# First MLP of a two-layer decoder trunk: the relu's transpose moved from TensorE to VectorE and ScalarE

## What is computed

```python
def squared_relu_mlp(h, w_up, w_down):
    return jnp.square(jax.nn.relu(h @ w_up)) @ w_down      # 2048 -> 8192 -> 2048

for i in range(DEPTH):                                     # DEPTH = 2
    mod = (silu(c) @ w_ada[i] + b_ada[i])                  # 6 vectors of 2048
    sh_a, sc_a, g_a, sh_m, sc_m, g_m = split(mod, 6)
    h = x * (1 + sc_a) + sh_a
    y = mixer_i(h)                                         # differential / sliding-window attention
    x = layer_norm(ALPHA * x + (1 + g_a) * y)
    h = x * (1 + sc_m) + sh_m
    y = squared_relu_mlp(h, w_up[i], w_down[i])
    x = layer_norm(ALPHA * x + (1 + g_m) * y)
```

## Time and profile before

| | |
|---|---|
| median of 3 runs | 2228.99 us (2226.84 to 2229.18) |
| the profiled execution | 2228.67 us |
| its span | 2226.9 us |
| TensorE busy (PE) | 2168.5 us, 97% |
| VectorE busy (DVE) | 1790.6 us, 80% |
| ScalarE busy (ACT) | 981.3 us, 44% |
| HBM read | 592.60 MB |

### The profile page before, as it was taken

The page is one execution under the profiler, slowest core; times in us unless marked ns, Lnnn a source line. Parts: engine busy times, 40 slices in busy tenths (PEclk is TensorE's granted clock), DMA queues, the critical chain, the costliest instruction groups (busy, mean ns, idle before and its releaser), DMA issues.

```text
span 2226.9 us, 26022 instructions
## 1 busy us (share of the span) xinstructions
PE 2168.5 (97%) x9952; PEld 1791.8 (80%) x9952; DVE 1790.6 (80%) x2057; ACT 981.3 (44%) x1330; POOL 33.4 (2%) x53
## 2 busy tenths in 40 slices
PE   6999999999999999999999999999999999999997
PEld 6887888877888888888888788777888888888886
DVE  6899998887997897888786888777966865874877
ACT  1135444546433443443353655536534443443441
POOL 0001000000000000000000000000000000000000
PEclk9899999999999999999999999999999999999999
DMA  9999888877999999999985643365766676666663
GB/s 360 384 331 347 322 320 300 306 245 256 361 364 325 354 366 335 325 380 350 323 311 190 198 152 119 122 207 190 236 221 223 213 241 206 219 217 219 228 234 113
DMA packets 262592, 596.41 MB, mean 268 GB/s; under 512 B 13426, under 2 KB 14788, under 8 KB 262468
## 3 DMA queue, kind: packets, MB, share of 16 engines
q1 hardware_dynamic: 254800, 579.45, 74.2%
q10 hardware_dynamic: 7668, 15.30, 2.2%
HBM read 592.60 MB, written 2.10 MB: 267 GB/s over the span
## 4 chain that ended last, share of the span: by engine, by line
PE 88%; DVE 7%; DMA 1%; issue 1%; ACT 1%; SPq 0%; DVEq 0%; POOL 0%; ACTq 0%; POOLq 0%
PE pair L1709 25%; PE pair L1711 25%; PE pair L1710 25%; DVE acc L916 2%; DVE w_lo L901 1%; PE pair L1967 1%; PE pair L1969 1%; PE pair L1968 1%; PE pair L1729 1%; PE pair L1731 1%; PE pair L1730 1%; PE turn L2041 1%; DMA y<-in_w_ada_dram 1%; PE turn L2022 1%; PE turn L1603 1%
## 5 line engine op out<-in xcount | busy, mean ns | idle before, releaser
L528 ACT ACTIVATE w_hi<-raw 128x1024 fp32r<-128x1024 f32 x712 | 726.8, 1056 | 620.2 <-PE pair L1711 297.4
L901 DVE TENSOR_TENSOR w_lo<-raw,w_hi 128x1024 fp32r<-128x1024 f32 x712 | 852.5, 1220 | 117.0 <-ACT w_hi L528 110.8
L1709 PE MATMUL pair<-w_hi,h_hi 128*128 128x512 f32 x1456 | 581.3, 399 | 1.5 <-DVE w_lo L901 0.8
L1711 PE MATMUL pair<-w_hi,h_lo 128*128 128x512 f32 x1456 | 567.8, 390 | 0.0
L1710 PE MATMUL pair<-w_lo,h_hi 128*128 128x512 f32 x1456 | 567.3, 390 | 0.0
L1709 PE MATMUL pair<-w_hi,f_hi 128*128 128x512 f32 x1056 | 414.0, 392 | 0.1
L1711 PE MATMUL pair<-w_hi,f_lo 128*128 128x512 f32 x1056 | 411.1, 389 | 0.0
L1710 PE MATMUL pair<-w_lo,f_hi 128*128 128x512 f32 x1056 | 410.9, 389 | 0.0
L929 DVE SCALAR_TENSOR_TENSOR acc<-ada_w,cvec,acc 128x1024 f32<-128x1024 f32 x300 | 383.6, 1279 | 1.8 <-DVE x L1312 0.9
L1709 PEld LDWEIGHTS pair<-w_hi,h_hi 128*128 128x128 f32 x1456 | 273.5, 188 | 62.9 <-DVE w_lo L901 6.3
L1711 PEld LDWEIGHTS pair<-w_hi,h_lo 128*128 128x128 f32 x1456 | 273.2, 188 | 58.4
(11 more groups left out here) (190 smaller groups left out, 1669.5 us busy)
## 6 DMA issues: line engine op xcount, KB each, us to landing
ada_w<-in_w_ada_dram SPq DMA_DIRECT2D x320, 512.0 KB, 6.1
raw<-in_w_up_dram SPq DMA_DIRECT2D x128, 1024.0 KB, 6.1
raw<-in_w_down_dram SPq DMA_DIRECT2D x128, 1024.0 KB, 5.2
raw<-in_a_w_qkv_dram SPq DMA_DIRECT2D x48, 1024.0 KB, 7.6
ada_f<-in_w_ada_dram SPq DMA_DIRECT2D x44, 512.0 KB, 11.5
raw<-in_b_w_qkv_dram SPq DMA_DIRECT2D x20, 1024.0 KB, 5.2
raw<-in_a_w_o_dram SPq DMA_DIRECT2D x16, 1024.0 KB, 6.5
raw<-in_b_w_o_dram SPq DMA_DIRECT2D x16, 1024.0 KB, 5.1
```

Source lines behind the costliest of these rows:

```text
L528: act.activation(w_hi[:, (b.n * SUB + n) % SPLITS], raw[:, slot, k:k + 2], ACT.Copy).then_inc(hi_ready, 1)
L901: dve.tensor_tensor(w_lo[:, slot, k:k + 2], raw[:, slot, k:k + 2], w_hi[:, (b.n * SUB + n) % SPLITS].bitcast(F32), ALU.subtract).then_inc( ...
L1709: pe.matmul(o, hi[:, kt, at], w[:, k], start=kt == 0, stop=False)
L1711: mm = pe.matmul(o, lo[:, kt, at], w[:, k], start=False, stop=kt == KT - 1)
```

## The change

In layer 0 the relu is now transposed without TensorE, in a third way. ScalarE writes the relu to `R` as before. VectorE turns all of it with one instruction, 128x1024, from `R` into the PSUM tensor `turn[:, 0]` (`up_turn`, behind its `split_lo(2)`); every 32x32 square is turned in place. ScalarE then copies sixteen quarter-rows of 32x256 from there to `RR`, which brings the squares to their partitions: eight behind `split_hi(3)`, eight behind `split_hi(4)` (`up_move`), and squares from `RR` behind `split_hi(5)` (before: behind `split_hi(4)`). VectorE's difference stands behind `split_lo(5)` (before: `split_lo(4)`), the relu behind ScalarE's `split_hi(2)` (before: 1). TensorE's `turn_up` is gone.

The modulation pieces of the first MLP follow a table over 31 steps: 4 in each of the first four, 7 or 8 in the four steps with results of down blocks, 6 in the steps with results of up blocks of the later rounds, 4 in the last three. The sums are complete at the steps 4, 7, 9, 11, 14, 16, 18, 21, 23, 25, 28 and after the end (before: 3, 5, 7, 10, 12, 14, 17, 19, 21, 24, 26, 28); only the first ten need an insert on TensorE within the MLP. The table of the second MLP gives the same pieces and sums as the rule did.

```diff
-ON_CHIP = (1,)
+ON_CHIP = (0, 1)
+BY_SCALAR = (0,)
@@
-MLP_BLOCKS = 28
-MLP_ADA = {1: [5], 2: [1, 5], 4: [1, 3, 5, 7], 5: [0, 1, 3, 5, 7], 6: [0, 1, 3, 5, 6, 7], 7: [0, 1, 3, 4, 5, 6, 7]}
+MLP_ADA = {0: [], 1: [5], 2: [1, 5], 4: [1, 3, 5, 7], 5: [0, 1, 3, 5, 7], 6: [0, 1, 3, 5, 6, 7],
+           7: [0, 1, 3, 4, 5, 6, 7], 8: [0, 1, 2, 3, 4, 5, 6, 7]}
+MLP_PIECES = (4 * [4] + [7, 8, 7, 8] + 2 * (4 * [6] + [7, 8, 8, 8]) + 4 * [6] + 3 * [4],
+              [(i + 1) * 32 // 28 - i * 32 // 28 for i in range(28)] + 3 * [0])
@@
-def mlp_pieces(i, halves):
-
-    return (MLP_ADA[(i + 1) * 16 * halves // MLP_BLOCKS - i * 16 * halves // MLP_BLOCKS] if i < MLP_BLOCKS else [])
-
-
-def mlp_sum(i, halves):
-
-    return {-(-MLP_BLOCKS * (k + 1) // halves): k for k in range(halves)}.get(i)
+def mlp_pieces(layer, b):
+
+    return MLP_ADA[MLP_PIECES[layer][b]]
+
+
+def mlp_sum(layer, b):
+
+    before, after = sum(MLP_PIECES[layer][:b - 1]) // KT, sum(MLP_PIECES[layer][:b]) // KT
+    return before if b > 0 and after > before else None
@@ ScalarE
+            def up_move(first, last):
+
+                def run():
+                    act.wait_ge(up_blocks, st.turned.n + 1)
+                    for i in range(first, last):
+                        a, c = i // 4, i % 4
+                        ins = act.activation(by_token(rows32(up_rows(RR), c), a),
+                                             by_feature(rows32(turn[:, 0], a), c), ACT.Copy)
+                    if last == 16:
+                        ins.then_inc(up_moved, 1)
+                return run
@@ ScalarE, mlp
                     if layer in ON_CHIP:
+                        if i < 4 and layer in BY_SCALAR:
+                            hk[3], hk[4] = up_move(0, 8), up_move(8, 16)
                         if i < 4:
                             hk[5] = up_square_there(i)
@@ VectorE
+            def up_turn(b, pp):
+
+                dve.wait_ge(evacuated, b + 3)
+                dve.transpose(turn[:, 0], up_rows(R)).then_inc(up_blocks, 1)
@@ VectorE, mlp
                     if layer in ON_CHIP and i < 4:
-                        hooks[3] = up_turn_rest
-                        block_(before=up_turn_across, later=(5, up_rest(i)), ada=mlp_pieces(b, halves), hooks=hooks)
+                        if layer not in BY_SCALAR:
+                            hooks[3] = up_turn_rest
+                        block_(before=up_turn if layer in BY_SCALAR else up_turn_across, later=(5, up_rest(i)), ada=mlp_pieces(layer, b), hooks=hooks)
```

More of the change, by code:

```diff
@@ L498, in mlp @@
                     src = up(it, i + 1) if i < 3 else down(it, i - 3) if i < 7 else up(it + 1, 0)
-                    load_block(src, mlp_pieces(b, 2 * len(parts)), of)
+                    load_block(src, mlp_pieces(layer, b), of)
             mlp(0)
@@ L802, in mlp @@
                     for half in range(2):
-                        if mlp_sum(b + 2, halves) == gate_at + half:
+                        if mlp_sum(layer, b + 2) == gate_at + half:
                             hk[0] = load_gate_bias(layer, 5, half)
@@ L1462, in mlp @@
                     last = it == QUARTERS - 1
-                    k = mlp_sum(b, halves)
+                    k = mlp_sum(layer, b)
                     hooks = {}
@@ L1472, in mlp @@
                     if layer in ON_CHIP and i < 4:
-                        hooks[3] = up_turn_rest
-                        block_(before=up_turn_across, later=(5, up_rest(i)), ada=mlp_pieces(b, halves), hooks=hooks)
+                        if layer not in BY_SCALAR:
+                            hooks[3] = up_turn_rest
+                        block_(before=up_turn if layer in BY_SCALAR else up_turn_across, later=(5, up_rest(i)), ada=mlp_pieces(layer, b), hooks=hooks)
                         continue
                     block_(before=(down_last if last else down_add)(i - 4) if i >= 4 else None,
-                           later=(4, up_lo(i)) if i < 4 else None, ada=mlp_pieces(b, halves), hooks=hooks)
+                           later=(4, up_lo(i)) if i < 4 else None, ada=mlp_pieces(layer, b), hooks=hooks)
             mlp(0, 1, 0)
```

## The result

| | before | after |
|---|---|---|
| median | 2229.06 us | 2252.41 us (2250.76 to 2253.29) |
| profiled execution | 2228.67 us | 2252.58 us |
| its span | 2226.9 us | 2250.8 us |
| TensorE busy | 2168.5 us | 2166.4 us, 96% |
| VectorE busy | 1790.6 us | 1810.4 us, 80% |

The kernel is slower by 23.4 us: ratio 1.011, 95% interval 1.0098 to 1.0122. The forecast was 2252.5.

What follows compares the result with a forecast made beforehand. TensorE, never dry, was taken as the bound. Removed inserts save 14.4 us, but a VectorE-ScalarE loop longer than the block makes it 38.2 us late: 2228.7 + 23.8 = 2252.5 us, range 2238 to 2268.

Steps and rivals of the forecast that it cites:

- What bounds the kernel, and what goes away: TensorE never runs dry; removing its 16 relu-turn inserts of 0.90 us in the first MLP saves 14.4 us.
- The transpose: VectorE's new 128x1024 transpose from SBUF into PSUM after each up block: 1.25 us, between 1.14 and 1.79.
- The dearer rival: VectorE's transpose into PSUM takes 1.79 us, adding 8.6 us for 2261 us; chance 0.08.
- The copies: ScalarE's sixteen 32x256 copies per up block, held by changing start partitions: 0.40 us apart, bounds 0.27 and 0.42.
- ScalarE's side: First part of the transpose-to-transpose loop: transpose, hand-over, sixteen copies, two splits and squares, 11.76 us.
- the blocks' lateness: TensorE's delay in first-MLP blocks because the loop of 24.6 us exceeds the 21.76 us block: 38.2 us together.
- runs 2, 3 and 4: Groups of four first-MLP blocks after up blocks, with modulation sums; predicted late by 9.2, 9.6 and 8.3 us.
- VectorE's side: Rest of the loop, f_lo and everything queued before the next transpose: 12.8 us, 13.1 in the first four blocks.
- The idle time ahead of L1709: TensorE's waits at a subtile's first matmul line, some 30 to 40 us, all for VectorE's w_lo.
- The DMA: Loads for down blocks with eight pieces: 0, bounds 0 and +8 us; rival that it fails, 2260 us, chance 0.05.
- the residual: VectorE's residual work in the first MLP's last down blocks: 0.7 us more lateness after run 4.
- overlapping copies: Rival: ScalarE's copies start 0.28 us apart, runs late by only 7 us, 2221 us; break-even about 0.307; chance 0.07.

Runs made afterwards that it cites:

- the kernel with both edits: Against the kernel after: up-block modulation pieces moved into VectorE's waits, and the last three steps' pieces 6, 6, 0 instead of 4, 4, 4; 2214.37 us (0.9935).
- the kernel with the same rows: Against the kernel after: four copies in a row keep input and output partitions, so most copy wrong squares; 2229.4 us (1.0005).

## Why the prediction was right, and where it was not

- **What bounds the kernel, and what goes away:** right. 14.4 us for the sixteen inserts: the kernel with both edits has the pieces and the chain hidden and is 14.3 below before.
- **The transpose,** taken at 1.25: sixteen rows of 1.249 to 1.260. The dearer rival is out.
- **The copies,** taken at 0.40 apart: 0.388 on the mean (925.42 - 922.34 = 3.08 and 929.63 - 926.51 = 3.12 for eight). The step was right in kind, held by the start partition, and read off two neighbours of ScalarE with 64 partitions; its size was 0.012 too large. ScalarE's side is 11.57 instead of 11.76: 0.19 in sixteen loops, 3.0 of the 3.7 by which the blocks' lateness was overrated. Another part I had not looked for: a sum begins with the cheaper L943, 0.5 less, which falls into the loop once in each of runs 2, 3 and 4, 1.6 together. In run 4 some of it goes again, since its first transpose starts 1.57 after its block instead of the 1.26 that I took; about 0.6 us of difference is left that is not assigned.
- **VectorE's side,** 12.8 by counting its queue: 12.26 with the cheaper piece, 12.80 without. Waits of 2 to 3 us in the fifth and sixth subtile: 1.92 and 2.98.
- **The idle time ahead of L1709 (now L1732),** foretold as 30 to 40 us: 24.8 for w_lo by the page, 32.0 by starts. The mechanism is there; the rows leave out 0.27 of each wait, as shown above.
- **The DMA,** taken at 0 with up to 8: nothing. The down blocks with 7 and 8 pieces are 21.76 without an insert, in the kernel after as in the one with the table alone.
- **The missing term.** The prediction moved pieces into the last three steps and counted nothing there, except 0.7 for the residual. In the last block, by half steps, w_lo has no lead and VectorE's queue passes two more jobs (L1166, L1168) between them: a piece ahead of a w_lo that TensorE waits for is paid there, and behind the longer wait the clock is lower. Every kernel here with pieces on the last step has both the wait of 3.3 us and the lower clock, and none of the others has either; which of the new wait and the longer one the clock needs was not separated. Together +4.1, and the expectation that single waits stay at 2 us or less and the granted clock at 1 was wrong there. An error of -3.7 and one of +4.1 cancelled: the total of 2252.5 against 2252.41 is closer than the working deserved.
- **The rivals:** overlapping copies would have given 2221 by my sum; the kernel that has them took 2229.4, or 2225.3 without the missing term. Their size was off too: I had eight of them as 8 x 0.28 = 2.24, and the rows of the kernel with the same rows have 2.38 and 2.41 from the first copy to the instruction behind the eight (930.44 to 932.82, 933.90 to 936.31), since the fifth copy is still held by the fourth and what starts behind the eight by the last. That is 0.31 a loop, at most 5 us in sixteen, about the 4 that are missing. Per copy it is a mean of 0.299, at which this change is worth nothing (ratio 1.0005); my sum, which had no missing term, put that point at 0.307.

## What to carry to other kernels

When a job goes off the busiest engine onto two others as a chain (A, then B, then A again), compare the block with the loop, and not with the busy shares: both helpers had room (83% and 55%), and the block was 24.7 instead of 21.76. The remedy is not less work but its place: filler that has no due time belongs behind the instruction at which its engine is going to wait, here a second table of places, 35 us. And look where such filler has no lead to eat, a block by half steps at the end of a stage.

## What was new about the chip

- ScalarE overlaps two copies of 32x256 (0.36 to 0.37 long, 0.27 to 0.28 apart) only if they start in the same partition on input and on output. If either changes, or both, they are 0.37 to 0.39 apart, no less than the 0.37 to 0.38 that one takes.
- VectorE's transpose of 128x1024 from SBUF into PSUM takes 1.255 us and lets the next pass start after 1.16 to 1.17, hardly more than its other passes of that size (1.22, 1.14).
- Waits of TensorE of 1.4 to 1.9 us, and one of 2.7 (with the old spread of pieces, 626.27 to 629.01), left the granted clock at 1.00. With one of 3.3 us it fell in all five kernels that have it, in the kernel after about 1 us after the matmuls had resumed, to a mean of 0.53 over 3.6 us. In the kernel with the table alone it fell before they had resumed, and 6 us at 0.51 followed: the last block is 4.1 us longer in one program and 5.3 in the other.
